# Decode layer on one core: rows of h ahead of the positions, slots signalled by tile, wider products, page numbers in later lots

## The reference

```python
h = modulate(rms_norm(x), sh1, sc1)
parts = split_cols(h @ w_in)
o_a = moba_attention(...)          # top-3 blocks of 256 keys and the own one
br = nsa_attention(...)            # compressed, selected and window branch
x = x + g1 * ((m_a * (o_a @ w_br_a) + m_b * (o_b @ w_br_b)) @ w_out)
h2 = modulate(rms_norm(x), sh2, sc2)
# hmoe: top-1 of 4 groups, then top-2 of its 8 experts
p_grp = softmax(t @ w_grp); g_sel = argmax(p_grp)
top_v, top_i = top_k(softmax(le_g), 2); top_v = top_v / sum(top_v)
act = silu(a) * b * combine
x = x + g2 * einsum('nef,efd->nd', act, w_eout)
y = rms_norm(x, norm_final_g)
```

## Time and profile before

| | |
|---|---|
| Median of three runs | 800.25 us (796.86 to 800.35) |
| Profiled execution, its own time | 802.13 us |
| Its span | 800.3 us |
| TensorE busy | 713.0 us (89%) |
| VectorE busy | 262.4 us (33%) |
| ScalarE busy | 170.8 us (21%) |
| GpSimd busy | 79.9 us (10%) |
| Mean granted TensorE clock | 0.968 of full |
| Read from HBM / written | 230.52 MB / 19.67 MB |

### The profile page before, as it was taken

How to read it: one execution, slowest core, us unless ns; L and a number is a source line. 1 busy time by engine, 2 the same in 40 slices (tenths; PEclk the granted TensorE clock), 3 DMA queues, 4 the chain that set the end, 5 groups by cost and what they waited for, 6 DMA issues and landing times.

```text
span 800.3 us, 12266 instructions
## 1 busy us (share of the span) xinstructions
PE 713.0 (89%) x4544; PEld 381.9 (48%) x4544; DVE 262.4 (33%) x872; ACT 170.8 (21%) x410; POOL 79.9 (10%) x118
## 2 busy tenths in 40 slices
PE   2979999999999999979787999989999988777765
PEld 2625666555466666534435776654433322222233
DVE  0144333201100278766442232376412111111126
ACT  0222344211100255423223000231101101100102
POOL 0001000003300033410000000002121121111000
PEclk9989999999999999989999999989999999999987
DMA  7979976716235493189999995345999999999941
GB/s 241 399 306 425 377 308 231 304 64 255 85 112 218 162 390 140 53 299 382 393 391 389 406 424 223 132 145 205 360 420 419 416 420 417 419 420 419 410 158 66
DMA packets 59043, 236.17 MB, mean 295 GB/s; under 512 B 9227, under 2 KB 17428, under 8 KB 43940
## 3 DMA queue, kind: packets, MB, share of 16 engines
q1 hardware_dynamic: 50420, 219.06, 69.5%
q0 software_dynamic: 6256, 14.18, 4.9%
q10 hardware_dynamic: 2304, 2.10, 0.9%
HBM read 230.52 MB, written 19.67 MB: 313 GB/s over the span
## 4 chain that ended last, share of the span: by engine, by line
PE 62%; SPq 20%; DMA 9%; DVE 5%; issue 3%; ACT 0%; DVEq 0%; POOLq 0%
PE bank L579 15%; SPq L450 7%; SPq L366 6%; PE bank L543 5%; PE bank L1060 5%; PE bank L952 4%; PE bank L968 4%; SPq L469 4%; DMA arena<-in_w_eout 4%; PE bank L526 3%; DMA arena<-in_v_pages 3%; PE bank L1082 3%; PE bank L626 3%; PE bank L702 2%; PE bank L551 2%
## 5 line engine op out<-in xcount | busy, mean ns | idle before, releaser
L1060 PE MATMUL bank<-arena 128*32 128x512 f32 (+1 forms) x928 | 117.9, 607 | 17.2 <-DMA arena<-in_w_ein 17.2
L579 PE MATMUL bank<-arena 128*128 128x320 f32 x448 | 124.2, 433 | 0.0
L579 PEld LDWEIGHTS bank<-arena 128*128 128x128 f32 x448 | 83.6, 189 | 40.3 <-issue 6.4
L1060 PEld LDWEIGHTS bank<-arena 128*32 128x32 f32 (+1 forms) x928 | 32.4, 114 | 92.0 <-issue 65.9
L1082 PE MATMUL bank<-arena 128*32 128x512 f32 (+1 forms) x464 | 58.3, 595 | 8.1 <-DMA arena<-in_w_eout 7.7
L1872 DVE COPY arena<-bank 128x512 f32<-128x512 f32 x14 | 9.7, 692 | 106.4 <-PE bank L1040 106.4
L543 PE MATMUL bank<-arena 128*128 128x512 f32 x96 | 42.7, 595 | 0.0
L1361 ACT ACTIVATE arena<-bank 128x256 f32<-128x256 f32 x16 | 6.2, 385 | 154.6 <-PE bank L1060 154.6
L968 PE MATMUL bank<-arena 128*128 128x320 f32 x128 | 35.0, 432 | 0.0
L952 PE MATMUL bank<-arena 128*128 128x320 f32 x128 | 35.0, 433 | 0.0
L1188 ACT ACTIVATE arena<-bank 32x320 f32<-32x320 f32 x60 | 25.7, 429 | 41.5 <-PE bank L579 40.9
(11 more groups left out here) (397 smaller groups left out, 939.4 us busy)
## 6 DMA issues: line engine op xcount, KB each, us to landing
arena<-in_w_ein SPq DMA_DIRECT2D x52, 1024.0 KB, 25.6
arena<-in_w_eout SPq DMA_DIRECT2D x26, 1024.0 KB
arena<-in_w_ada SPq DMA_DIRECT2D x12, 2048.0 KB, 11.3
arena<-in_w_in SPq DMA_DIRECT2D x10, 2048.0 KB, 9.9
arena<-in_k_pages SPq DMA_DIRECT2D x64, 320.0 KB, 6.4
arena<-in_v_pages SPq DMA_DIRECT2D x64, 320.0 KB, 10.1
arena<-in_w_ein SPq DMA_DIRECT2D x3, 4096.0 KB, 22.1
arena<-in_cmp_pages SPq DMA_DIRECT2D x48, 128.0 KB, 5.9
```

Of the source, the lines that this page charges most:

```text
L579: m = mm(banks[c % 4][:, 0:N], ring[q][:, k, P * (c % 4):P * (c % 4 + 1)], hT[:, k, :], start=(k == 0), stop=(k == KD - 1))
L1060: m = mm(banks[2 + p % 2][r:r + n, :], xeT[p % 2][:, k, r:r + n], wi2[p % 3][:, e, k, :], start=(k == 0), stop=(k == KD - 1))
```

## The change

Four edits. The parts 6 and 7 of h go ahead of the position products. `first_slots` is signalled tile by tile, and TensorE waits for each tile. VectorE masks the logits in one product over all tiles, and writes `first` and `second` with one product each. SP reads the page numbers of round 3 in two lots of eight, behind `keys(2)` and behind `values(1)`.

```diff
-            def page_ids(i):
+            def page_ids(i, b):
-                return [[page_of(2 * i + b, p) for p in range(PAGES)] for b in range(2)]
+                return [page_of(2 * i + b, p) for p in range(PAGES)]
...
-            ids = [page_ids(0), None, None]
+            ids = [[page_ids(i, b) if i == 0 else None for b in range(2)] for i in range(3)]
...
             keys(0)
             values(0)
-            ids[1] = page_ids(1)
-            ids[2] = page_ids(2)
+            for i in (1, 2):
+                for b in range(2):
+                    ids[i][b] = page_ids(i, b)
             keys(1)
-            ids[0] = page_ids(3)
             for i in range(1, 4):
                 if i < 3:
                     keys(i + 1)
+                if i == 1:
+                    ids[0][0] = page_ids(3, 0)
                 values(i)
+                if i == 1:
+                    ids[0][1] = page_ids(3, 1)
...
-            h_rows_of(4, 6)
+            h_rows_of(4, 8)
             te.wait_ge(s_m, 1)
...
-            h_rows_of(6, 8)
-            te.wait_ge(s_m, 2)
             for t in range(4):
+                te.wait_ge(s_m, 2 + t)
                 te.wait_ge(s_hr, 2 * t + 2)
...
-            te.wait_ge(s_m, 3)
+            te.wait_ge(s_m, 6)
...
-                te.wait_ge(s_m, 4)
+                te.wait_ge(s_m, 7)
...
-            for t in range(4):
-                m = ve.tensor_tensor(big[R, t], lg[R, t, 4:36].rearrange("p (g e) -> p e g", e=8),
-                                     oh[R, t].unsqueeze(1).to_broadcast([RT, 8, 4]), ALU.mult)
-            link(m)
+            link(ve.tensor_tensor(big[R], lg[R, :, 4:36].rearrange("p t (g e) -> p t e g", e=8),
+                                  oh[R].unsqueeze(2).to_broadcast([RT, 4, 8, 4]), ALU.mult))
...
             for ch, o in ((first, oh1), (second, oh2)):
-                for t in range(4):
-                    m = ve.tensor_tensor(ch[R, t].rearrange("p (g e) -> p g e", e=8), o[R, t].unsqueeze(1).to_broadcast([RT, 4, 8]),
-                                         oh[R, t].unsqueeze(2).to_broadcast([RT, 4, 8]), ALU.mult)
+                m = ve.tensor_tensor(ch[R].rearrange("p t (g e) -> p t g e", e=8), o[R].unsqueeze(2).to_broadcast([RT, 4, 4, 8]),
+                                     oh[R].unsqueeze(3).to_broadcast([RT, 4, 4, 8]), ALU.mult)
...
             for t in range(4):
-                m = ve.scalar_tensor_tensor(first_slots[R, t], slots_here, rowE[R, 4 + t:5 + t], first_slots[R, t], ALU.is_equal, ALU.add)
-            m.then_inc(s_m, 1)
+                ve.scalar_tensor_tensor(first_slots[R, t], slots_here, rowE[R, 4 + t:5 + t], first_slots[R, t], ALU.is_equal, ALU.add)\
+                    .then_inc(s_m, 1)
```

## The result

The changed kernel is slower: 805.73 us (median of 10 runs) against 800.38 for the kernel before (10 runs), a ratio of 1.006 with a 95% interval of 1.0035 to 1.0085. I had forecast 799.5 in 796.4 to 802.5. The profiled execution took 810.38 us, its span is 808.6, and the mean granted clock over it 0.956.

A forecast was written before the change was run, and what follows sets the result against it. DMA traffic bounds two stretches; the second's start hangs on the router chain through TensorE and VectorE. Router gain 0.67 and pages 0: 800.25 - 0.7 = 799.5 us, own range 797.5 to 801, 8 in 10 runs 796.4 to 802.5.

The forecast's parts named there:

- What the clock takes back: Slot matmuls (L1021): the idle gap before them lowers the clock, losing 2.1 us (1.65 to 2.95) of 2.77 gained.
- the second rival: Low clock lasts through all slot matmuls, up to +4.4 us, perhaps another queue hole; priced +2.5, 802.7 us; chance 0.12.
- Wide products: VectorE in the router: four products become one (0.29 us), eight become two (0.50); 0.68 us less, all on the chain.
- Rows ahead: TensorE: parts six and seven fit before the wait for `chosen`; positions run at full clock, gaining 0.87 us (0 to 1.03).
- Signal by tile: Slot matmuls start after VectorE's first tile, 2.77 us earlier with the other router edits; later tiles are never late.
- Pages: SP's page-number reads in two later lots: 0.77 us gained at the keys, a hole against it; taken as 0 (-0.6 to +0.8).
- The hole of 0.6 us: Page traffic before the values of round 1: the queue runs dry 0.6 us, eating most of the 0.77 gained.
- The second lot: Eight page-number reads behind `values(1)`: hidden by queued traffic, with 1.2 us in hand.
- The chain: From the slot matmuls through the tables and VectorE to the second pair: an earlier L1021 end moves the end equally.

The follow-up runs named there:

- e6: Kernel before, with all 16 page numbers of round 3 read ahead of `keys(1)`; 797.63 us against 801.05, ratio 0.997.
- e1: Kernel before, with only parts 6 and 7 of h moved ahead of the positions; 806.24 us against 799.78.
- e8: Changed kernel, with slot matmuls over all 128 rows in place of 80; 800.01 us against 801.05 for the kernel before.
- e2: Changed kernel, with parts 6 and 7 of h back behind the positions; 796.49 us against 799.78 for the kernel before.
- e4: Kernel before, with only the page numbers of round 3 read in two later lots; 798.62 us against 799.78, ratio 0.9972.
- e3: Changed kernel, with three unused 128x512 filler products behind the positions; 796.13 us against 799.78 for the kernel before.
- e5: Kernel before, with only the wide VectorE products and the signal by tile; 800.63 us against 801.05.
- e7: Changed kernel, with filler behind the positions and round 3's page numbers read ahead of `keys(1)`; 796.36 us against 801.05 for the kernel before, 0.9946.

## Why the prediction was wrong

**The step that failed is "What the clock takes back".** I took 2.1 us, bounds 1.65 and 2.95, from low stretches of 5.9 and 3.3 us. Measured is a low stretch of 20.5 us that took 5.76 at the slots and 1.56 at the tables, and 0.82 more ahead of the second pair: 8.1 us in place of 2.1. The outcome is the second rival, which I gave 0.12 and priced at +2.5; its mechanism was right, and its price stopped at the end of L1021, where the low level went on through L1026 and into the hidden layer. Its own upper bound, +4.4, was also too low for this trace's +5.3; over the nine runs the loss is 4.8 us by the ratio (2.8 to 6.8). That the clock falls only when L1021 already runs was right, and it did not help: the fall came 1.0 us into it, and then nothing ended the low level.

The fault was in how I read the earlier trace rows. Both short stretches ended in products over 128 rows: parts six and seven in the first, the hidden layer in the second. I took the length of a low stretch for a property of the gap. In these traces it went with what ran behind it. In the kernel before the clock came back during part seven, at 534.5, just in front of L1021 (in e6 again so, at 533.5); moved ahead, parts six and seven could not do that, and in e1 the slots then stayed at 0.50 for all of their 13.8 us. The second stretch, from 544.9, wasn't even one behind a gap: TensorE had been busy without a pause since 528.77, and what ran in front of it were the slot matmuls and the tables. The end stage's 9 us at 0.50 with TensorE busy, which I had used for the rival alone, was the better guide. The Trainium skill ("TensorE: Matmul & The Clock Gate", Part 1) calls the throttled state the default and says that activity releases it; here TensorE was busy 12.89 of 12.90 us and stayed at 0.54. The measurement decides: busy was not enough. In e8, with products over 128 rows, the clock was back after 3.4 us.

**Whether the clock falls at a gap varies.** In front of the positions, gaps of 2.65 (e2) and 3.23 us (e4) did not lower it, gaps of 3.24 did in the kernel before and in e6. In front of the second pair six of the profiles have the same gap of 2.66 or 2.67 us: a stretch of 3.4 us at 0.50 followed it in e3, e4 and e8, whose hidden layer there took 8.78 (e8: 8.54) us, and none in e2, e5 and e7, where it took 7.09. The run-to-run variation that the Trainium skill states, weighed in the prediction, is seen here at the start of a low stretch. It does not excuse my bound: the mean over nine runs is 58 us low in the changed kernel against 40 over 28 and 35 of the kernel before, so the dear outcome was no rare one.

How much of such low time lies on the path can't be told from the means. The profiles say it better: from part five to the second pair the changed kernel stands 8.1 us behind e3 (35.00 - 26.93), which differs by the filler alone, and 9.0 were measured by the ratios; e1 stands 6.7 behind the kernel before, and 6.6 were measured.

**Wide products: nearly right.** L1861 took 0.49 for 0.50 forecast. L1841, which also reads the logits in another order than they lie, took 0.38 for 0.29, so the gain is about 0.6, not 0.68.

**Rows ahead: half right.** The parts fit in front of the wait, and the positions ran at 1.00 in 1.2 us, as forecast; e1 starts its slots 8.14 us after part five for 9.64 before, a gain of 1.5. But e4 has the same 8.13 with the parts left in place and the clock up, and e2 shows what I had not asked: with parts six and seven left behind the positions the slots start after the same 6.8 us. The edit had nothing to give whenever the clock holds in front of the positions, and much to lose.

**Signal by tile: right.** With all edits the slots start 2.86 us sooner against part five, forecast 2.77, and TensorE, busy 12.89 of 12.90 us, never waits for a later tile. The signal's own part is about 0.8: e2 starts its slots 1.37 us sooner than e4, of which 0.6 belongs to the wide products.

**Pages: too low.** Forecast 0 (-0.6 to +0.8), measured -2.2 (e4) and -2.4 (e6) by the ratios. The earlier issue came as counted (0.75 us in e4 for 0.77). The hole of 0.6 us did not open in e4 (387 GB/s from 372 to 380, 389 before). In the changed kernel, with the same reads at the same place, 359 stood there, which is 0.6 us' worth of traffic less; why it dips in one and not in the other is open. The second lot hid behind the traffic as forecast (393 GB/s from 380 to 387 in the changed kernel). The stretch behind 355 us also filled faster in e4, 261 and 376 GB/s against 214 and 361 before. What of the rest is traffic and what chance isn't settled; the intervals reach from 0.8 to 3.8 (e4) and from 0 to 4.8 (e6).

**The chain held.** The second pair follows the tables' end as before (11.98 us for 11.16), and what this profile had lost by then came out at the end: 7.7 us late at the second pair, 8.3 in the span. One reading of mine was loose: from 519 on the chain runs over VectorE and ScalarE and not over TensorE alone, which changes nothing in the sum.

## What to carry to other kernels

Before work is moved ahead of a wait, ask what the tensor engine will do after it: dense products that stood between an idle gap and a light phase may be what keeps that phase at full clock. A few filler products in the gap (here 2.82 us, off the chain) were worth 1.1% of the changed kernel. Price a fall of the clock by the work that follows it, up to products like those that ended such a stretch elsewhere in the trace, and not by the length of another stretch.

## What the hardware showed unexpectedly

64 products of 80 rows by 128 columns ran back to back for 13.1 us, all but the first 1.0 at 1.2 GHz, and 16 of three columns for 3.3 more, without the clock coming back; the same 64 over 128 rows had it back after 3.4 us. In e1 the low level lasted for 13.8 us of slots as well and ended near 552, again only in the hidden layer.

The clock also fell with no idle gap ahead. In the kernel before, TensorE was busy without a pause from 528.77 to 553.9, and it fell near 544.8, 0.7 us into the hidden layer and behind 8.9 us of slots and tables:

```profile
543.00:544.00 1.00, 1.00 (x11) 1.00 (x10) 0.00 (x0) 0.59 (x2) 0.54 (x1) 1.00 0.00 0
544.00:545.00 1.00, 1.00 (x6) 0.41 (x7) 0.74 (x6) 0.00 (x0) 0.00 (x0) 0.88 0.00 0
```

It did so in e6 too (near 543.7), and not in e2, e3, e4, e5 and e7, whose first hidden layer took 7.09 us for 8.78. Gaps of the same length ended some with and some without a fall: 3.23 and 3.24 us in front of the positions, 2.66 and 2.67 us in front of the second pair.
